# Turning the fourth token tile inside the first filler product, later waits for its last copies, and one weight rounding between the exponentials

## The reference, cut to what matters

```python
x = layer_norm(ALPHA * x + m, ln_g[layer, 0], ln_b[layer, 0])
c = memory_cross_attention(x, mem, x_wq[layer], x_wkv[layer], x_wo[layer])
x = layer_norm(ALPHA * x + c, ln_g[layer, 1], ln_b[layer, 1])
f = swiglu(x, f_w_up[layer], f_w_down[layer])
x = layer_norm(ALPHA * x + f, ln_g[layer, 2], ln_b[layer, 2])
```

```python
r = sigmoid(einsum(xb, wa) + ba);  i = sigmoid(einsum(xb, wx) + bx)
log_a = -LRU_C * r * softplus(-lam);  a = exp(log_a);  mult = sqrt(-expm1(2.0 * log_a))
h_t = a_t * h_(t-1) + mult * (i * xc);   y = h * gelu(gate);   out = y @ w_out
```

## Time and profile before

| | us |
|---|---|
| median of three runs | 1537.52 |
| the profiled execution, its own time | 1531.01 |
| its span | 1529.2 |
| PE busy in it | 1501.4 |
| ACT, DVE, POOL busy | 611.0, 547.6, 667.1 |

### The profile page before, as it was taken

One profiled execution on the slowest core, in us unless ns is written; L12 is line 12 of the kernel. 1 busy time (PEld: TensorE's weight loads), 2 busy tenths in 40 slices (PEclk: granted clock), 3 DMA queues, 4 the chain that ended last, 5 costly groups with the idle time before them and its releaser, 6 DMA issues.

```text
span 1529.2 us, 21541 instructions
## 1 busy us (share of the span) xinstructions
PE 1501.4 (98%) x7906; PEld 1268.4 (83%) x7906; DVE 547.6 (36%) x918; ACT 611.0 (40%) x1222; POOL 667.1 (44%) x530
## 2 busy tenths in 40 slices
PE   8999999999999999999999999999999999999998
PEld 7889998888888888888887867788888888888886
DVE  2753555454372101110006188845444111011014
ACT  3345554344443323332233468734433333233221
POOL 5542122532455444444464543554243444444442
PEclk9999999999999999999999999999999999999999
DMA  9331112321234333333232522332122332333222
GB/s 240 94 97 55 33 39 80 110 97 56 90 95 143 92 103 97 97 91 103 97 121 86 152 80 66 109 118 97 56 90 97 97 98 89 105 97 99 97 97 90
DMA packets 115714, 147.05 MB, mean 96 GB/s; under 512 B 20534, under 2 KB 74160, under 8 KB 115632
## 3 DMA queue, kind: packets, MB, share of 16 engines
q1 hardware_dynamic: 115312, 145.87, 31.0%
q0 software_dynamic: 320, 0.08, 0.0%
HBM read 143.80 MB, written 2.10 MB: 95 GB/s over the span
## 4 chain that ended last, share of the span: by engine, by line
PE 93%; DVE 3%; ACT 2%; issue 1%; DMA 0%; POOL 0%; SPq 0%; DVEq 0%; ACTq 0%
PE ps L648 83%; PE ps L873 3%; PE ps L653 2%; PE ps L853 2%; PE ps L837 1%; DVE h L1705 1%; DMA x_res<-in_x 0%; PE ps L798 0%; DVE h L1731 0%; PE ps L930 0%; POOL w_lo L612 0%; PE ps L829 0%; DVE ib_alt L1730 0%; DVE h L1738 0%; ACT ra L1314 0%
## 5 line engine op out<-in xcount | busy, mean ns | idle before, releaser
L612 POOL TENSOR_TENSOR w_lo<-w_raw,w_hi 128x512 fp32r<-128x512 f32 (+2 forms) x468 | 601.4, 1293 | 833.2 <-ACT w_hi L1073 830.3
L1073 ACT ACTIVATE w_hi<-w_raw 128x512 fp32r<-128x512 f32 (+2 forms) x468 | 280.4, 612 | 549.1 <-PE ps L648 539.1
L648 PE MATMUL ps<-fm_hi,w_hi 128*128 128x512 f32 (+1 forms) x1112 | 423.2, 381 | 7.2 <-POOL w_lo L612 5.3
L648 PE MATMUL ps<-fm_lo,w_hi 128*128 128x512 f32 (+1 forms) x1112 | 420.0, 378 | 0.0
L648 PE MATMUL ps<-fm_hi,w_lo 128*128 128x512 f32 (+1 forms) x1112 | 419.9, 378 | 0.0
L648 PEld LDWEIGHTS ps<-fm_hi,w_hi 128*128 128x128 f32 x1112 | 210.0, 189 | 48.6 <-POOL w_lo L612 7.3
L648 PEld LDWEIGHTS ps<-fm_lo,w_hi 128*128 128x128 f32 x1112 | 210.1, 189 | 38.7 <-issue 0.7
L648 PEld LDWEIGHTS ps<-fm_hi,w_lo 128*128 128x128 f32 x1112 | 209.8, 189 | 38.9
L1866 DVE TENSOR_TENSOR gf<-silu,ps 128x512 f32<-128x512 f32 x44 | 28.3, 684 | 417.4 <-ACT silu L1406 399.7
L1613 DVE SCALAR_TENSOR_TENSOR x_res<-x_res,ps 128x512 f32<-128x512 f32 x48 | 31.4, 686 | 273.1 <-PE ps L648 187.8
L648 PE MATMUL ps<-w_hi,g_hi 128*128 128x512 f32 x288 | 112.0, 389 | 0.0
(11 more groups left out here) (280 smaller groups left out, 2213.5 us busy)
## 6 DMA issues: line engine op xcount, KB each, us to landing
w_raw<-in_f_w_up SPq DMA_DIRECT2D x352, 128.0 KB, 2.1
w_raw<-in_f_w_down SPq DMA_DIRECT2D x88, 256.0 KB, 2.6
w_raw<-in_x_wkv SPq DMA_DIRECT2D x48, 256.0 KB, 3.1
w_raw<-in_o_w_in SPq DMA_DIRECT2D x40, 256.0 KB, 2.6
w_raw<-in_x_wq SPq DMA_DIRECT2D x32, 256.0 KB, 2.7
w_raw<-in_x_wo SPq DMA_DIRECT2D x32, 256.0 KB, 2.8
w_raw<-in_e_w_in SPq DMA_DIRECT2D x24, 256.0 KB, 2.9
w_raw<-in_o_w_out SPq DMA_DIRECT2D x20, 256.0 KB, 2.6
```

The costliest lines, as they stand in the source:

```text
L612: nc.gpsimd.tensor_tensor(lo[:, :n], w_raw[:, c % RING, :n], hi[:, :n].bitcast(F32), ALU.subtract).then_inc(w_split, 1)
L648: last = nc.tensor.matmul(outp, lhsT, rhs, start=(clear and k == 0 and n == 0), stop=(k == steps - 1 and n == 2), skip_group_check=True)
L1073: nc.scalar.activation(w_pair(c)[0][:, :n], w_raw[:, s, :n], ACT.Copy).then_inc(w_rounded, 1)
```

## The change

`product` can be given a range of chunks, and `evacuated` can be told to wait for one copy fewer (`but=1`). In `turn_late` the first filler is cut after four chunks (RING is 4): tile 3 is turned there. In ACT's `norm` the roundings before the copies of tile 3 become two (filler chunks 4 and 5); the five others follow after. Where another product follows, PE waits behind the turn for all copies of tile 3 but the last on each of ACT and DVE, and for the last ones at chunk 4 (`last_tile_turned`). In `decays` one rounding is put after the exponentials of half of the set's tiles.

```diff
-            def evacuated(name, m=0):
+            def evacuated(name, m=0, but=0):
                 if ACT_AFTER[name]:
-                    pe.wait_ge(evac_a, ACT_AFTER[name] + PAIR_EVACS * m)
+                    pe.wait_ge(evac_a, ACT_AFTER[name] - but + PAIR_EVACS * m)
                 if DVE_AFTER[name]:
                     late = name[:2] == "ln" and name[-1] == "0"
-                    pe.wait_ge(evac_d, DVE_AFTER[name] - late + PAIR_EVACS * m)
+                    pe.wait_ge(evac_d, DVE_AFTER[name] - late - but + PAIR_EVACS * m)
...
                 for name, feature_major in fillers[:1]:
-                    product(name, mem, MEM, feature_major)
+                    product(name, mem, MEM, feature_major, chunks=(0, RING))
                 turn_normed(l, i, 3)
                 if following:
                     early_half(following, RING - 1, RING)
+                    evacuated(f"ln{l}{i}_1", but=1)
+                for name, feature_major in fillers[:1]:
+                    product(name, mem, MEM, feature_major, chunks=(RING, KT))
                 for name, feature_major in fillers[1:]:
                     product(name, mem, MEM, feature_major)
-                evacuated(f"ln{l}{i}_1")
+                if not following:
+                    evacuated(f"ln{l}{i}_1")
+
+            def last_tile_turned(l, i):
+                return lambda k: evacuated(f"ln{l}{i}_1") if k == KT // 2 else None
...
-                product(f"q{l}_0", fm, SEQ, True, early=RING)
+                product(f"q{l}_0", fm, SEQ, True, early=RING, ready=last_tile_turned(l, 0))
...
-                    product(f"up{l}_{n}", fm, SEQ, True, early=0 if n else RING * l)
+                    product(f"up{l}_{n}", fm, SEQ, True, early=0 if n else RING * l,
+                            ready=last_tile_turned(1, 1) if l and not n else None)
...
                 if fillers:
-                    round_weights(following + KT + RING - 1)
+                    round_weights(following + RING + 2)
                 if turns:
                     turned_copies(3)
...
+                            if j == tiles // 2 - 1:
+                                round_on(1, meanwhile)
```

## The result

The changed kernel took 1524.02 us in the median of six runs (1523.36 to 1530.23), the kernel before beside it 1535.79 (1531.81 to 1537.78). The ratio is 0.9939, 95% interval 0.9914 to 0.9964: faster by 0.61%. (It is the ratio of the means; the two medians alone would give 0.9923.) The forecast was 1531.9, 0.36% faster, with a range of 1527.5 to 1536.0.

The account below looks back on a forecast made before the run. PE was taken to bound the kernel, busy 1501.4 of 1529.2 us, so only its waits could shrink. Gains 3.1 + 0.6 + 1.85 = 5.55, taken as 5.6 off the median 1537.52, gave 1531.9 us; range 1527.5 to 1536.0.

Parts of the forecast that it names:

- Part A: First fillers of norms (0,1) and (0,2): two 2.06 us waits go, small new waits come; gain 3.1, bounds 2.0 and 4.1.
- 0.2 for chunk 11: Second norm's first filler: 0.2 us allowed because chunk 11 is rounded behind the copies of the filler's result.
- Part B: Later waits for tile 3's last copies: 0.6 us gained at up1_0, none at q0_0 and q1_0; between 0 and 1.9.
- Part C: Recurrent block, roundings moved amid the exponentials: gain 0.7 + 1.15 = 1.85 us, bounds 3.4 and -1.35.
- The cap at chunk 3 of oout0: Recurrent block: chunk 3 is rounded as late as before, so PE's 3.4 us is not kept; new wait about 1.6.
- the first set: Oin2 in the recurrent block: 1.1 us from earlier splits, another 0.6 if the clock stays up; taken as 1.4.
- the reserve of 0.7: Oout0: chunk 3 was split at 991.4 and needed at 992.1, so 0.7 us of PE's 3.4 stays.
- 1 (no cap): Oout0's weights come in time after all: C 3.4, sum 7.1, time 1530.4 us; chance 0.20.
- 2 (fillers starve): Late landings starve the fillers: A 2.0, sum 4.45, time 1533.1 us; chance 0.20 shared with rival 5.
- 3: DVE's lock loss isn't returned: C -1.35, sum 2.35, time 1535.2 us; chance 0.12, including a C near 0.
- 4: Roundings amid exponentials delay DVE and ACT by 5.0 us at the y tile: slower, 1539.6 us; chance 0.06.
- 5: Tile 3 normalised after PE's fourth filler chunk: A is 3.1 less that delay; chance 0.20 shared with rival 2.

Follow-up runs that it names:

- e3: Only the later waits for tile 3's last copies, put on the kernel before: 1532.64 us, ratio 0.9995.
- e4: Only the rounding amid the exponentials, put on the kernel before: 1530.38 us, ratio 0.998.
- e9: The kernel before, unedited, profiled once more: 1532.05 us.
- e10: The kernel before, unedited, one further profiled execution: 1531.71 us.
- e2: The change with only its filler part kept, the other two parts taken back: 1527.37 us, ratio 0.9955 against the kernel before.
- e11: The kernel before with two more waited-for copies on ScalarE ahead of tile 3's copies in the two norms with fillers: 1536.00 us, ratio 1.002.
- e7: The changed kernel with chunk 4 of q0_0 and q1_0 rounded after six of eight key and value roundings: 1522.74 us, ratio 0.9937 against the kernel before.
- e5: The changed kernel with chunk 3 of oout0 rounded ahead of the third set's first y tile: 1522.38 us, ratio 0.993 against the kernel before.
- e1: The changed kernel again, no edit: 1524.30 us against 1532.96 for the kernel before, ratio 0.9945.
- e6: The changed kernel with chunks 6 and 7 of oin2 rounded behind the first set's first and second tiles: 1523.65 us, ratio 0.9945 against the kernel before.
- e12: The changed kernel with chunk 4 of q0_0 and q1_0 and chunks 3 and 4 of oout0 rounded earlier: 1521.70 us, ratio 0.9936 against the kernel before.

## Why the prediction was wrong in time and right in most of its mechanism

**Part A.** Forecast 3.1, measured 1.84 + 1.71 = 3.55 in the trace (waits of 0.20 and 0.30, and no 0.2 for chunk 11), and more in the runs. The mis-sized term is the price of the two waits that go: I put them at their 2.06 us of idle time each, and the half clock behind them at nothing. In five profiled executions that have these waits (before, e3, e4, e9, e10) four of ten ended in half clock, for 1.47, 1.61, 1.61 and 1.59 us: 1.26 an execution on average, a rough figure from four events (the three profiles of the unedited kernel alone give two of six and 1.07). The earlier trace rows had shown half clock behind an idle time of 2.93; I priced it where I saw it and not where a like wait stood that had been spared in the one execution that I read. e2 and e11 move this term in both directions.

**Part B.** 0.6 at up1_0 and nothing at q0_0 and q1_0, as forecast; e3 shows it alone, and e7 shows that the place behind ACT's eight roundings is what holds the other two. The waits at chunk 4 came as 0.52, not 0.6.

**Part C.** Forecast 1.85, 1.33 between the first two profiles. The cap at chunk 3 of oout0 was real (a wait of 1.41, forecast 1.6), and e5 lifts it. What was mis-sized is the first set, at 1.4: the way from the first gate product to the gate products behind oin2 shrank from 33.64 to 32.98, by 0.66. The forecast had a win there if the clock stayed up; it was at half for 3.4 us, as before. The gelu of oin2 comes with PE, so DVE's wait for it shrank by 0.66 too, from 1.23 to 0.57, and its chain gained 0.69 until the y tile (988.13 less 982.53, less the 4.91 by which the gate products come earlier), not 1.15. This chain sets when chunk 3 of oout0 is rounded: 0.69 and the reserve of 0.7 make the 1.4 that were measured. DVE lost nothing by the moved splits. Windows of DVE from the first gate product to that y tile, before and with the change:

```profile
893.59:988.13 94.54, 82.54 (x85) 0.98 0.27 81
```

```profile
888.68:982.53 93.85, 82.52 (x84) 0.98 0.27 82
```

But the block as it was takes 135.33 to 137.31 in six profiles (before, e2, e3, e9, e10, e11; mean 136.1), and with the rounding 134.00 to 134.21 in four (the changed kernel, e1 with 134.13, e4, e7; mean 134.1): 2.0 on average. The two longest of the six, e2 and e11, are those in which the half clock lasted 6.8 us; without them it is 1.5. So part of C, too, hung on the clock of the one execution that I read.

**The sum.** 3.55 + 1.26 + 2.0 + 0.6 = 7.4 (6.9 with 1.5 for C), against 7.8 between the medians of e1. The 0.4 to 0.9 left are not explained.

**The step that failed most** is the one behind the sum: "I take the difference off the median: 1537.52 - 5.6". Of 66 executions of the kernel before (e9 and e10 not counted), 50 lie between 1529.26 and 1535.06 with a median of 1532.0, and 16 between 1537.08 and 1539.84; two of the three that I started from were of the upper part, and so was their median; the profiled execution, 1531.01, was one of the lower. The difference had been worked out from the one and was taken off the other. Off the profiled execution it gives 1525.5. Of the error of 7.9 us 6.4 is this. Of the other 1.5, 1.3 is in the difference of the two profiles: 1.34 ahead of norm (0,0) and 0.45 more of part A, less 0.52 of part C; the last 0.1 to 0.2 was not looked for. That 1525.5 comes so near is in part luck: the profiled execution had lost 1.3 us at half clock ahead of norm (0,0), which about made up for the filler clock (1.26 on average) that it was spared. Windows of PE, the first profile of before and e9:

```profile
12.00:16.00 4.00, 4.00 (x26) 0.67 0.66 183
```

```profile
12.00:16.00 4.00, 4.00 (x36) 1.00 0.67 190
```

**The rivals.** 1 (no cap): wrong, 1.41 at oout0. 2 (fillers starve): wrong, 0.20 and 0.30. 3 and 4 (DVE loses, slower): wrong; e4 is 1.7 us faster alone. The exclusive lock of the Trainium skill (SBUF — State Buffer, "Who interferes with whom") agrees again with the trace, 1.78 us beside POOL against 0.69 alone. The lower bound for C did not come all the same: DVE is busy for 82.52 us up to the y tile where it was for 82.54, so the moved splits cost it nothing in sum, and the 0 net of the prediction was right. 5: wrong, the turn comes at 441.50 and waits for nothing.

The signs that the prediction listed came in kind. Three were smaller than said: 0.20 at chunk 6 of k1_0 (0.3 to 0.5), 0.52 at chunk 4 of q0_0 and q1_0 (0.6 to 0.7), and 1.41 at oout0 (1.6).

## What to carry to other kernels

Price a wait of the matrix engine by its idle time, up to 0.3 us more that the view doesn't show (e7), and the half-clock stretch that may follow, also where the one profiled execution was spared it; a second and third profile of the same kernel show how often it comes. Take a difference off the execution from which it was worked out, and read the single times before trusting a median of three. Time won ahead of an engine stays only as far as the next engine in the chain was waiting for it (0.5 of 3.5 us in e6). Compare stage by stage, between instructions with no wait at them: a stage in which nothing is changed and the clock stays up agrees within 0.05 us here, so a term of 0.6 us can be read from a profile that timed runs don't resolve (e3: 0.9995 [0.998, 1.0011]).

## What the runs showed of the hardware

- After the same idle time PE's clock may fall or not: behind 2.06 us in four of ten cases. Behind the pair of 0.30 and 2.03 to 2.04 us in oin2 it fell in the changed kernel, e1, e4, e7 and e12, and in e5 it didn't. Behind 3.31 us it fell in both cases, behind 2.93 us in all six. It came back by itself while PE worked on.
- When it falls varies as well: behind 2.06 us between 0.5 us (e4) and 1.4 us (e3) after PE had resumed; with 3.31 us it was down at once in one of two cases (e11, 452.10); with 2.03 us it was down before PE resumed (changed kernel, 911.20).
- Behind the same wait of 2.93 us the half clock lasted 3.4 us in four profiles (before, e3, e9, e10) and 6.8 us in two (e2, e11).
- It also fell without an idle time worth the name: 13.8 us at 0.51 amid small matrix products (e3, 150.5), where PE's longest wait was 0.26; it cost 6.5 us in that execution. What releases it stays open. If it stands behind all the long executions, which only this one profile bears out, it comes in about a quarter of those of the kernel before and in three of 13 of the changed one.
